# A two-layer attention and FFN kernel: narrow products and transposes spread between wide products, and a second 128-byte pad

## The reference

```python
for layer in range(2):
    u = rmsnorm(h, mix_pre_g[layer])
    if layer == 0:
        proj = u @ ab_w_in[0]            # latents of MLA, and q, k, v of MoBA
        mla_out = mla_attention(...)     # 8 heads, causal softmax, rope
        moba_out = moba_attention(...)   # 8 heads, softmax with a distance bias
        mixed = concat([mla_out, moba_out]) @ ab_w_out[0]
    else:
        qkv = u @ sb_w_qkv[0]            # 16 heads
        mixed = stick_breaking_attention(q, k, v) @ sb_w_out[0]
    h = h + rmsnorm(mixed, mix_post_g[layer])
    gu = rmsnorm(h, ffn_pre_g[layer]) @ ffn_w_gate_up[layer]
    f = (silu(gu[..., :2816]) * gu[..., 2816:]) @ ffn_w_down[layer]
    h = h + rmsnorm(f, ffn_post_g[layer])
```

## Time and profile before

| | |
|---|---|
| median of three runs | 1331.95 us (1331.87 to 1332.46) |
| the profiled execution | 1332.39 us, of which 1330.6 us are the span from its first to its last instruction |
| PE busy | 97% of the span, 6599 matmuls |
| DVE, ACT, POOL busy | 55%, 42%, 20% |
| mean granted clock of PE | 0.989 |

### The profile page before, as it was taken

How to read it: one execution, slowest core, us unless ns; L and a number is a source line. 1 busy time by engine, 2 the same in 40 slices (tenths; PEclk the granted TensorE clock), 3 DMA queues, 4 the chain that set the end, 5 groups by cost and what they waited for, 6 DMA issues and landing times.

```text
span 1330.6 us, 17696 instructions
## 1 busy us (share of the span) xinstructions
PE 1291.9 (97%) x6599; PEld 1093.1 (82%) x6599; DVE 734.3 (55%) x998; ACT 554.5 (42%) x885; POOL 260.1 (20%) x205
## 2 busy tenths in 40 slices
PE   6989999999999999999999999999999999999997
PEld 5677788898888888888888888887988888888886
DVE  4777654538644454422288787776574455443223
ACT  5456665546322223322354555454453322223112
POOL 1532200025211111100051111320441111110002
PEclk9989999999999999999999999999999999999999
DMA  5412222122333333333222111311223333332331
GB/s 163 132 43 71 65 72 72 48 79 81 111 95 95 99 101 96 87 101 96 83 79 65 48 48 52 90 48 47 81 81 110 95 95 95 95 112 93 95 96 63
DMA packets 190503, 112.34 MB, mean 84 GB/s; under 512 B 13696, under 2 KB 184773, under 8 KB 190446
## 3 DMA queue, kind: packets, MB, share of 16 engines
q1 hardware_dynamic: 188636, 106.81, 27.6%
q0 software_dynamic: 640, 2.10, 0.5%
q10 hardware_dynamic: 1170, 2.66, 0.5%
HBM read 109.43 MB, written 4.74 MB: 86 GB/s over the span
## 4 chain that ended last, share of the span: by engine, by line
PE 85%; DVE 8%; ACT 3%; issue 2%; POOL 1%; DMA 0%; POOLq 0%; ACTq 0%; SPq 0%; DVEq 0%
PE banks L433 26%; PE banks L435 25%; PE banks L434 25%; PE banks L1712 3%; DVE w_lo L428 1%; PE banks L1742 1%; PE banks L1630 1%; PE banks L1459 1%; DVE logits L1421 1%; PE banks L482 1%; DVE tf L702 1%; ACT logits L1432 1%; DVE probsT_lo L1471 1%; POOL stick_lo L1729 0%; DVE u_lo L712 0%
## 5 line engine op out<-in xcount | busy, mean ns | idle before, releaser
L428 DVE TENSOR_TENSOR w_lo<-w_raw,w_hi 128x1024 fp32r<-128x1024 f32 (+3 forms) x200 | 288.0, 1443 | 264.9 <-ACT w_hi L421 264.7
L433 PE MATMUL banks<-u_hi,w_hi 128*128 128x512 f32 (+1 forms) x1112 | 424.9, 382 | 5.8 <-DVE w_lo L428 4.3
L435 PE MATMUL banks<-u_hi,w_lo 128*128 128x512 f32 (+1 forms) x1112 | 419.1, 377 | 0.0
L434 PE MATMUL banks<-u_lo,w_hi 128*128 128x512 f32 (+1 forms) x1112 | 418.9, 377 | 0.0
L421 ACT ACTIVATE w_hi<-w_raw 128x1024 fp32r<-128x1024 f32 (+3 forms) x200 | 206.0, 1031 | 277.0 <-PE banks L435 277.0
L433 PEld LDWEIGHTS banks<-u_hi,w_hi 128*128 128x128 f32 x1112 | 210.2, 189 | 45.7 <-issue 4.9
L435 PEld LDWEIGHTS banks<-u_hi,w_lo 128*128 128x128 f32 x1112 | 210.1, 189 | 38.8
L434 PEld LDWEIGHTS banks<-u_lo,w_hi 128*128 128x128 f32 x1112 | 210.3, 189 | 37.8 <-issue 1.0
L905 POOL TENSOR_TENSOR up<-up,gate 128x512 f32<-128x512 f32 x44 | 71.8, 1632 | 375.2 <-DVE up L931 358.4
L886 ACT ACTIVATE gate<-gate 128x512 f32<-128x512 f32 x44 | 27.8, 632 | 202.3 <-DVE gate L927 202.3
L1729 POOL TENSOR_TENSOR stick_lo<-softplus,stick_hi 128x1280 fp32r<-128x1280 f32 x14 | 44.1, 3164 | 156.9 <-DVE stick_hi L1725 156.9
(11 more groups left out here) (256 smaller groups left out, 1987.5 us busy)
## 6 DMA issues: line engine op xcount, KB each, us to landing
w_raw<-in_ffn_w_gate_up_dram SPq DMA_DIRECT2D x88, 512.0 KB, 3.6
w_raw<-in_ffn_w_down_dram SPq DMA_DIRECT2D x30, 512.0 KB, 3.6
w_raw<-in_sb_w_qkv_dram SPq DMA_DIRECT2D x24, 512.0 KB, 3.6
w_raw<-in_ab_w_in_dram SPq DMA_DIRECT2D x17, 512.0 KB, 3.6
w_raw<-in_ffn_w_down_dram SPq DMA_DIRECT2D x16, 448.0 KB, 3.6
w_raw<-in_ab_w_out_dram SPq DMA_DIRECT2D x8, 512.0 KB, 3.8
w_raw<-in_sb_w_out_dram SPq DMA_DIRECT2D x8, 512.0 KB, 4.5
bias_by_distance<-bias_rows ACTq DMA_DIRECT2D x1, 2560.0 KB
```

The costliest lines, as they stand in the source:

```text
L428: dve.tensor_tensor(wl[:, c.slot, 0:w], raw[:, c.slot, 0:w], wh[:, c.slot, 0:w].bitcast(F32), ALU.subtract).then_inc(w_lo, 1)
L433: nc.tensor.matmul(o, lh, rh, start=start, stop=False, skip_group_check=True)
L434: nc.tensor.matmul(o, lh, rl, start=False, stop=False, skip_group_check=True)
L435: return nc.tensor.matmul(o, ll, rh, start=False, stop=stop, skip_group_check=True)
```

## The change

It does four things.

1. In `values`, `scores_pe`, `c_pe`, `sb_pv_pe` and `z_pair_pe` the narrow matmuls, which stood behind one another at the end of a strip or of the stage, stand one by one behind wide matmuls that write other columns. Generators hand them out: `mm3` takes one after each of its three matmuls.
2. In even steps of layer 0 one transpose of the probabilities is issued, then slot a with one transpose behind each of its matmuls, then what is left of the transposes. Odd steps keep all ten together.
3. A tile `latent_line_pad` of 128 bytes stands behind `rden`.
4. The semaphores that tell of the end of a stage move to the matmul that is now last; their counts stay as they are.

The number of matmuls, their shapes and operands are the same. No instruction of DVE, ACT, POOL or SP moves in its own list.

```diff
@@ -221,6 +221,7 @@
             rden = sb(at0, "rden", [P, 2, TT])
+            sb(at0, "latent_line_pad", [P, 32])
@@ mm3, project, item_pe @@
-        def mm3(o, lh, ll, rh, rl, start, stop):
+        def mm3(o, lh, ll, rh, rl, start, stop, narrow=iter(())):
             nc.tensor.matmul(o, lh, rh, start=start, stop=False, skip_group_check=True)
+            next(narrow, None)
             nc.tensor.matmul(o, lh, rl, start=False, stop=False, skip_group_check=True)
-            return nc.tensor.matmul(o, ll, rh, start=False, stop=stop, skip_group_check=True)
+            next(narrow, None)
+            mm = nc.tensor.matmul(o, ll, rh, start=False, stop=stop, skip_group_check=True)
+            next(narrow, None)
+            return mm
...
-                mm = project(pe, b[0:m, :], c, KQ, 2 * MLA_QH, e * HD, m, cqh, cql)
+                mm = project(pe, b[0:m, :], c, KQ, 2 * MLA_QH, e * HD, m, cqh, cql, narrow=narrow)
@@ scores_pe @@
-            for i in (3, 1, 2, 0):
+            def first_tile():
+                o = SC[:, ROW_AT[0]:ROW_AT[0] + P]
+                for lq, rk in ((qh, kh), (qh, kl), (ql, kh)):
+                    mm = nc.tensor.matmul(o, lq[:, 0:P], rk[:, 0:P], start=False, stop=lq is ql, skip_group_check=True)
+                    if lq is ql:
+                        mm.then_inc(sc_done, 1)
+                    yield
+
+            for i in (3, 1, 2):
                 w, at, q = P * (i + 1), ROW_AT[i], slice(i * P, (i + 1) * P)
                 mm = mm3(SC[:, at:at + w], qh[:, q], ql[:, q], kh[:, 0:w], kl[:, 0:w],
-                         start=(i != 0), stop=True)
+                         start=True, stop=True, narrow=first_tile() if i == 2 else iter(()))
@@ probs_pe @@
-            mm.then_inc(pt_done, 1)
+                    if j == TT - 1:
+                        mm.then_inc(pt_done, 1)
+                    yield
@@ values @@
+            def last_block():
+                o, at = out_bank[:, P * (TT - 1):T], COL_AT[TT - 1] + at0
+                for lv, rx in ((v[0], xh), (v[0], xl), (v[1], xh)):
+                    nc.tensor.matmul(o, lv[:, buf, TT - 1, cols], rx[:, at:at + P], start=False, stop=False,
+                                     skip_group_check=True)
+                    yield
+
+            for j in range(TT - 1):
...
+                         narrow=last_block() if j == 0 else iter(()))
@@ z_pair_pe @@
-            for j in (0, 1, 3, 2):
+            for blocks in ((0,), (1,), (2, 3)):
                 for n, (lhs, rhs) in enumerate(Z_TERMS):
-                    for e in range(2):
-                        z_block(par, e, j, lhs, rhs, j != 3 and n == 0)
+                    for j in blocks:
+                        for e in range(2):
+                            z_block(par, e, j, lhs, rhs, j != 3 and n == 0)
@@ c_pe @@
+            narrow = last_blocks()
+            for j in range(TT - 1):
+                for jj in range(j, TT - 1):
+                    for n in (nsh, nsl):
+                        mm = block(j, jj, n)
+                        if (j, jj) != (0, 0) and (j, jj, n) != (TT - 2, TT - 2, nsl):
+                            next(narrow, None)
             mm.then_inc(c_done, 1)
@@ sb_pv_pe @@
-            for j in range(TT):
+            for j, n in ((0, 0), (3, 0), (0, 1), (3, 1), (1, 0), (1, 1), (2, 0), (2, 1)):
@@ the steps of layer 0 on PE @@
-                probs_pe(pe, hh)
-                item_pe(pe, a)
+                transposes = probs_pe(pe, hh)
+                next(transposes)
+                if hh % 2 == 0:
+                    item_pe(pe, a, transposes)
+                for _ in transposes:
+                    pass
+                if hh % 2:
+                    item_pe(pe, a)
```

More of the change, by code:

```diff
@@ L445, in project @@
                 last = mm3(o, wh[:, c.slot, s], wl[:, c.slot, s], xh[:, first + k, :], xl[:, first + k, :],
-                           start=(first + k == 0), stop=(first + k == total - 1))
+                           start=(first + k == 0), stop=(first + k == total - 1), narrow=narrow)
                 if inside and k == (kt // 2 - 1 if inside_at is None else inside_at):
@@ L1191, in head_of, with item_pe @@
             return 2 * it[1] + it[2]
-        def item_pe(pe, it):
+        def item_pe(pe, it, narrow=iter(())):
             if it is None:
@@ L1220, in item_pe @@
             else:
-                mm = project(pe, b, c, KD, P, 0, P, uh, ul)
+                mm = project(pe, b, c, KD, P, 0, P, uh, ul, narrow=narrow)
             mm.then_inc(w_used if last else pj_mm, 1)
@@ L1474, in values @@
         def values(out_bank, v, buf, e, xh, xl, at0):
-            for j in range(TT):
-                w, at, cols = T - P * j, COL_AT[j] + at0, slice(HD * e, HD * e + P)
+            cols = slice(HD * e, HD * e + P)
+            def last_block():
[5 more added lines that the diff above has]
+            for j in range(TT - 1):
+                w, at = T - P * j, COL_AT[j] + at0
                 mm = mm3(out_bank[:, P * j:T], v[0][:, buf, j, cols], v[1][:, buf, j, cols],
-                         xh[:, at:at + w], xl[:, at:at + w], start=(e == 0 and j == 0), stop=(e == 1 and j == TT - 1))
+                         xh[:, at:at + w], xl[:, at:at + w], start=(e == 0 and j == 0), stop=(e == 1 and j == TT - 2),
+                         narrow=last_block() if j == 0 else iter(()))
             return mm
@@ L1706, in c_pe, with block, last_blocks @@
             Z = ZB[e]
[L1707 to L1710, removed]
-                    for n in (nsh, nsl):
-                        mm = nc.tensor.matmul(Z[:, at:at + w], lt[:, :], n[:, e, COL_AT[jj]:COL_AT[jj] + w],
-                                              start=False, stop=False, skip_group_check=True)
+            def block(j, jj, n):
+                at, w = COL_AT[j] + (jj - j) * P, T - P * jj
+                return nc.tensor.matmul(Z[:, at:at + w], (negtri if jj == j else negones)[:, :],
+                                        n[:, e, COL_AT[jj]:COL_AT[jj] + w], start=False, stop=False,
+                                        skip_group_check=True)
+            def last_blocks():
+                for j in range(TT):
+                    for n in (nsh, nsl):
+                        yield block(j, TT - 1, n)
+            narrow = last_blocks()
[5 more added lines that the diff above has]
+                            next(narrow, None)
             mm.then_inc(c_done, 1)
@@ L1738, in sb_pv_pe @@
                 pe.wait_ge(so_read, p * 2 + 1)
-            for j in range(TT):
+            for j, n in ((0, 0), (3, 0), (0, 1), (3, 1), (1, 0), (1, 1), (2, 0), (2, 1)):
                 w, at = T - P * j, COL_AT[j]
[L1741 to L1744, removed]
+                mm = nc.tensor.matmul(bank(b)[:, P * j:T], sv[:, par, e, j, :], (swh, swl)[n][:, e, at:at + w],
+                                      start=(j == 0 and n == 0), stop=(j == 2 and n == 1), skip_group_check=True)
             mm.then_inc(sv_done, 1)
```

6 lines of the change are left out of this document (3 added, 3 removed).

## The result

The changed kernel takes 1337.46 us (median of 6 executions, 1335.81 to 1342.14), the kernel before 1332.24 (6, 1331.87 to 1332.79): ratio 1.0042, 95% interval 1.0026 to 1.0059. It is slower by 5.2 us; forecast were 3.4. The median lies 0.26 us above the forecast range. In a second set, on another chip, it took 1337.68 (5 executions) against 1333.41, ratio 1.0035 (1.0021 to 1.0049), so +4.3. The two sets agree within their intervals, and the loss is about 4.7 us.

A forecast was written before the change was run, and what follows sets the result against it. The prediction took PE to bound the kernel nearly everywhere, but DVE and ACT in layer 0's MLA steps. Narrow products 0, transposes' own time 0, late transposes +3.9, pad -0.5: +3.4 on 1331.95 gives 1335.4 us, range 1332.3 to 1337.2.

The forecast's parts named there:

- The step that failed: Layer 0, even steps 6 to 12: transposes 2.1 us late, taken in by ACT's 4.53 us idle; no cost.
- no new ones: Sign of being right: behind PE's longer wait near 100.9 us, the same PE waits as before and no new ones.
- Step 0: Layer 0's first step: item waits for the shared bank behind one transpose, transposes end late, `probsT_hi` 3.9 us later.
- the bank wait: Step 0: PE issues one transpose, then stands until 83.42 us for the shared bank; a new wait of 0.96 us.
- The term of +3.9: Step 0: clock stays at half, `probsT_hi` starts at 89.3 instead of 85.39, no slack behind; +3.9 us.
- The fall of the clock behind the grown wait: PE's wait at 96.98 us grows; if the clock falls behind it, some 1.5 to 2 us on top.
- the first rival: Step 0: clock rises on time, +2.2 - 0.5 = +1.7, 1333.7 us; chance 0.17 for this alone.
- Steps 2 and 4: Layer 0: 0.8 us bank wait goes into PE's 1.16 us wait for `mla_q_lo`; no cost.
- Narrow products: 277 narrow matmuls between wide ones: each still takes a 0.11 us slot; 0, with 0.7 us either way.
- the rival in which lone narrow products save 13.9 us: Loads reach further ahead; 277 narrow products cost their stream of 0.06 to 0.07 us, total 1321.5 us; chance 0.10.
- Pad: Second pad aligns `oB`, latents, MLA's and MoBA's q and k to 256 bytes; -0.5 us, between 0 and -1.0.
- Sum: Whole kernel: 0 + 0 + 3.9 - 0.5 = +3.4 us, giving 1335.4 us.

The follow-up runs named there:

- the first trace: Changed kernel, all parts of the change against the kernel before: trace of its longest execution, 1342.14 us.
- the earlier trace: Profiled execution of the kernel before, without the change: 1332.39 us.
- the 17 traces: All traces of the study: the kernel before, the changed kernel (two), and the follow-up kernels; no single time.
- all four traces: Those with nine transposes by turns in step 0: changed kernel twice (1342.14, 1336.05 us), kernel before with turns only (median 1338.38), changed kernel with turns in steps 0 to 4 (1337.16).
- the kernel without turns: Changed kernel with the transposes together in every step, other parts kept: 1332.85 us, ratio 0.9998 to the kernel before.
- the extra work: Kernel before with transposes issued again: four of step 12 1333.51 us; all of step 12 1335.22; steps 10, 12 1334.31; steps 8, 10, 12 1336.98.
- the parts: Changed kernel with transposes by turns only in steps 0 to 4 (1337.16 us), 6 to 10 (1335.72) or 12 (1336.14).

## Why the prediction was off

- **The step that failed**: "In steps 6 to 12 the transposes are 9 x 0.23 = 2.1 us late, but ACT stands idle for 4.53 us before the next exponentials and takes it in. No cost." It costs 2.4 us (shift against the kernel with transposes together: 2.59 to 4.99 between 150 and 254 us). The 4.53 us of ACT is time in which ACT waits for DVE's `neg_max`, and that hangs on the late transposes itself: `probsT_hi`, behind it `w_hi`, then `w_lo`, the scaling and the row maxima. The chain takes in 1.7 us of the 2.1 (0.9 of them gaps that the rows list), not 4.53; four waits for `v_lo` of 0.3 us follow. In step 12 the item's bank is read late as in step 0, which the forecast looked at in steps 0, 2 and 4 alone: 0.8 us. And a product and transpose by turns take 0.008 us more than apart, 0.3 in these steps. The forecast's "no new ones" among PE's waits fell with this step.
- **Step 0**: the mechanism was right, the bank wait (0.75 us against 0.96), the turns (0.64 us each against 0.63) and `probsT_hi` (88.69 against 89.3). The term of +3.9 was mis-sized by execution: it is +3.6 in the first trace (-0.18 to +3.40), where the clock was at half as in the earlier trace rows, and +1.5 where it is full. Of the 17 traces 14 have it full from 77 to 81 us on; the earlier trace rows were not the usual case. The fall of the clock behind the grown wait, which the forecast kept for its rivals, came in all four traces, +1.6. Together 3.1, or 5.2 in the first trace. That the term of 3.9 lies near 3.1 is in part luck: in three of the four traces with turns there it is made up as in the first rival (clock on time, wait grown, clock fallen behind it), to which the prediction gave 0.17, and not as in the forecast.
- **Steps 2 and 4**: no cost, as forecast.
- **Narrow products**: 0 with 0.7 either way was right. About +0.3 us in layer 0 (shift of the kernel without turns, 0.29 at 97 and 0.63 at 255 us) and -0.5 in the stick-breaking layer. One load ahead, begun with the product ahead, is what the rows show; the rival in which lone narrow products save 13.9 us fell.
- **Pad**: -0.5 was too much; -0.2 to -0.3. The products from oB went from 0.232 to 0.227 us. At the latents and the scores of MoBA no gain is shown.
- **Sum**: 3.1 + 2.4 - 0.2 - 0.2 = +5.1 by the traces, with falls of the clock in unchanged code that add or spare up to 1.5 us each; measured +5.2 and +4.3. Had steps 6 to 12 been priced, 3.4 + 2.4 = 5.8 would have been the forecast.

What stays open: what decides whether the clock falls at the norms near 308 and 960 us in a given execution, how often it does in each kernel, and with it whether the change or the extra work makes these falls more frequent.

## What to carry over

Idle time of an engine ahead of an instruction is slack only if what released it doesn't depend on the thing that is late; follow the releaser back, and add up what each link of that chain can take in. Work that stands ahead of an instruction covers its wait: when it is spread behind it, look for the wait in every step and not only in the first. Where one fall of the clock is worth as much as the effect, compare places in the traces as well as medians, since the medians of the parts (10.5 us here) can add up to more than twice the whole (4.7).

## What had not been expected of the hardware

A wait of 1.70 to 2.48 us near 100 us had half clock behind it in all four traces that have it, once with PE busy for 1.69 of the 3.40 us ahead, and cost 1.6 us beyond the wait itself; with 0.17 to 0.27 us there, none of 13 had it. And places of half clock worth up to 1.5 us moved in code that no edit touched: from 313.0, 681.6 and 964.9 us in one execution of the changed kernel to 904.4 in another, with PE's idle time near 308 us the same (0.74 and 0.76 us).
